# Another order for VectorE, ScalarE and GpSimd at both ends of the block products of a two-layer kernel

## The reference, cut to what matters

```
gate = sigmoid(x @ w_ple_gate)
x    = x + gate * (p_i @ w_ple_proj)
```

```
p = x @ w_in + b_in                     # a_u, a_v, q, k, v, r, a_low, g_a, g_b
v_n   = layer_norm(gelu(a_v))           # per token, over 1024 features
mixed = causal(w_s) @ v_n (per group of 128 features, chunks of 128 tokens) + b_s
y_a   = gelu(a_u) * mixed
log_f = log_sigmoid(a_low @ w_gate2 + b_gate) / 16
o     = gated linear attention(q, k, v, log_f), chunk by chunk
m     = sigmoid(g_a) * y_a + sigmoid(g_b) * norm(o) * silu(r)
h     = layer_norm(alpha * x + m @ w_out); then a feed-forward block of width 4096 with a second layer_norm
```

## Time and profile before

| | |
|---|---|
| median of 3 runs | 2411.16 us (2409.19 to 2412.22) |
| the profiled execution | 2408.89 us, span 2407.1 us |
| TensorE busy | 2324.1 us, 97% of the span, 12306 matmuls |
| weight loads (PEld) | 1884.6 us, 78% |
| VectorE | 1598.3 us, 66% |
| GpSimd | 1169.8 us, 49% |
| ScalarE | 890.7 us, 37% |
| mean DMA rate | 119 GB/s |
| mean granted TensorE clock | 0.986 of full speed |

### The profile page before, as it was taken

One profiled execution on the slowest core, in us unless ns is written; L12 is line 12 of the kernel. 1 busy time (PEld: TensorE's weight loads), 2 busy tenths in 40 slices (PEclk: granted clock), 3 DMA queues, 4 the chain that ended last, 5 costly groups with the idle time before them and its releaser, 6 DMA issues.

```text
span 2407.1 us, 33030 instructions
## 1 busy us (share of the span) xinstructions
PE 2324.1 (97%) x12306; PEld 1884.6 (78%) x12306; DVE 1598.3 (66%) x2066; ACT 890.7 (37%) x1383; POOL 1169.8 (49%) x699
## 2 busy tenths in 40 slices
PE   7999999999999997999899999999999999999996
PEld 5787777778888785778777877888877888888885
DVE  6657878876611648535677677646788666877788
ACT  4446454433200224453332232222263333444444
POOL 4355667673434535345323233344465555566665
PEclk9999999999999998999999999999999999999998
DMA  5333433436111352433222222222135444853322
GB/s 213 132 108 106 141 111 108 143 137 232 44 52 44 130 148 79 144 105 123 66 67 66 78 83 65 78 96 72 59 123 180 153 145 144 321 213 144 119 93 83
DMA packets 130087, 285.73 MB, mean 119 GB/s; under 512 B 13601, under 2 KB 49441, under 8 KB 125362
## 3 DMA queue, kind: packets, MB, share of 16 engines
q1 hardware_dynamic: 96672, 230.61, 27.6%
q10 hardware_dynamic: 33298, 53.56, 6.8%
HBM read 205.43 MB, written 78.72 MB: 118 GB/s over the span
## 4 chain that ended last, share of the span: by engine, by line
PE 45%; DVE 8%; issue 3%; DMA 2%; ACT 2%; POOL 1%; DVEq 0%; SPq 0%; ACTq 0%
PE pt L3702 15%; PE pt L3173 10%; PE wk L3702 6%; PE wk L3529 5%; PE pt L3529 3%; DMA eb<-o_d 1%; PE wk L3614 1%; PE wk L3713 1%; DVE darg L2708 1%; PE pt L3189 1%; DVE eb L2790 1%; PE wk L3647 1%; PE wk L3652 1%; PE wk L3648 1%; DVE ea L2792 0%
## 5 line engine op out<-in xcount | busy, mean ns | idle before, releaser
L833 POOL TENSOR_TENSOR w_hi<-w_raw,ones 128x1024 fp32r<-128x1024 f32 x70 | 137.0, 1957 | 548.1 <-PE pt L3173 510.5
L837 POOL TENSOR_TENSOR w_lo<-w_raw,w_hi 128x1024 fp32r<-128x1024 f32 x80 | 217.6, 2720 | 86.5 <-ACT w_hi L1107 65.5
L895 POOL TENSOR_TENSOR xl<-sraw,xh 128x512 fp32r<-128x512 f32 x80 | 137.5, 1729 | 81.0 <-ACT xh L1177 79.7
L976 POOL TENSOR_TENSOR wr_l<-raw,wr_h 128x512 fp32r<-128x512 f32 x80 | 137.1, 1717 | 79.5 <-ACT wr_h L1790 79.5
L3173 PE MATMUL pt<-h,w_hi 128*128 128x512 f32 x512 | 168.1, 410 | 1.2 <-DVE mix L2561 1.2
L3173 PE MATMUL pt<-l,w_hi 128*128 128x512 f32 x512 | 158.5, 391 | 0.0
L3173 PE MATMUL pt<-h,w_lo 128*128 128x512 f32 x512 | 158.3, 390 | 0.0
L948 POOL TENSOR_TENSOR l<-kq,h 128x512 fp32r<-128x512 f32 x64 | 88.5, 1393 | 112.7 <-ACT h L1481 112.7
L976 POOL TENSOR_TENSOR wr_l<-fraw,wr_h 128x512 fp32r<-128x512 f32 x60 | 79.9, 1335 | 90.9 <-ACT wr_h L1790 90.9
L3173 PE MATMUL pt<-xh,w_hi 128*128 128x512 f32 x384 | 119.5, 392 | 1.5 <-POOL w_lo L837 0.9
L3173 PE MATMUL pt<-xh,w_lo 128*128 128x512 f32 x384 | 118.7, 390 | 0.0
(11 more groups left out here) (667 smaller groups left out, 6755.0 us busy)
## 6 DMA issues: line engine op xcount, KB each, us to landing
w_raw<-ws_d SPq DMA_DIRECT2D x82, 512.0 KB, 3.5
fx_d<-stg SPq DMA_DIRECT2D x106, 256.0 KB, 2.8
sraw<-ws_d SPq DMA_DIRECT2D x32, 512.0 KB, 5.7
fraw<-ws_d SPq DMA_DIRECT2D x32, 512.0 KB, 5.0
raw<-ws_d SPq DMA_DIRECT2D x32, 512.0 KB, 8.7
kq<-ws_d SPq DMA_DIRECT2D x14, 1024.0 KB, 5.5
xs0f<-fx_d SPq DMA_DIRECT2D x10, 1024.0 KB, 4.9
xs1f<-fx_d SPq DMA_DIRECT2D x9, 1024.0 KB, 5.0
```

The costliest lines, as they stand in the source:

```text
L833: nc.gpsimd.tensor_tensor(out=w_hi[:, u, :], in0=w_raw[:, u, :], in1=zeros, op=ALU.add).then_inc(w_hi_done, 1)
L837: nc.gpsimd.tensor_tensor(out=w_lo[:, u, :], in0=w_raw[:, u, :], in1=w_hi[:, u, :].bitcast(f32), op=ALU.subtract).then_inc(w_split, 1)
L895: nc.gpsimd.tensor_tensor(out=lo, in0=sc_factor(n, SC_ORDER[i]), in1=hi.bitcast(f32), op=ALU.subtract).then_inc(sw_lo, 1)
L976: nc.gpsimd.tensor_tensor(out=low, in0=src, in1=high.bitcast(f32), op=ALU.subtract).then_inc(wl_done, 1)
```

## The change

No operation is added or removed, except that one wait of the mixing is taken at another count and three are added: ScalarE's last `eb` load and GpSimd's `split_pairs` now wait on `ln_ready`, and VectorE waits for its own last `mixed`. What moves:

- First seam, ScalarE: the load of `eb` for the last gate tile goes out when VectorE has read the old one; `quarter_hi(1)` and `(2)` stand ahead of `gate_high(KT - 2)`; `low_rank` stands ahead of all `piece_high`, and the loads of `wg2` are a function of their own behind `quarter_hi(11)`; `piece_high` and `quarter_hi` alternate.
- First seam, VectorE: the last gate tile is finished before `third_sum`; the first four `t_sum` stand before its low part; the memset of `alow` follows them; `t_sum` goes k by k; the rest of the sums is spread between the value steps.
- First seam, GpSimd: `second_low(k)` is spread between the weight lows 8 to 10.
- Logarithm units 0 and 1 are done at (2, 13) and (3, 7), the units 2 to 6 where 3 to 7 were, and unit 7 in product 13. The second operation of `z_min` is a function `z_less`, which for unit 0 is called later.
- Second seam: GpSimd's split waits for the first `norm_factors`; the memsets of `sc`, `kp` and `gst` stand before the mixing; the second half of the mixing takes the groups 4 to 7 first; and the first projection of the loop waits for the first ten groups that are emptied, not for all sixteen.

```diff
+LN_READY = 1
...
-    T_SUMS = [(n, 0) for n in ("T1", "T3", "T2", "T4")] + [(n, k) for k in range(1, 4) for n in ("T1", "T2", "T4")] + [
-        ("T3", k) for k in range(1, 4)]
+    MIXING = [(0, g) for g in range(KT)] + [(1, g) for g in (4, 5, 6, 7, 0, 1, 2, 3)]
+    T_SUMS = [(n, k) for k in range(4) for n in ("T1", "T3", "T2", "T4")]
...
         for g in range(28 * B_MATRICES):
+            if g == 8:
+                second_low(0)
+            if 8 <= g < 11:
+                second_low(g - 7)
             quarter_lo(g)
-            if g == 7:
-                for k in range(4):
-                    second_low(k)
+        pool.wait_ge(ln_ready, LN_READY + 1)
         split_pairs(S_G // 2, S_FF // 2)
...
-        def gate_load(i, u):
-            act.wait_ge(val_done, 3 * KT + i)
+        def gate_load(i, u, last=False):
+            act.wait_ge(*((ln_ready, 1) if last else (val_done, 3 * KT + i)))
...
         quarter_hi(0)
+        gate_load(KT - 1, 1, True)
+        quarter_hi(1)
+        quarter_hi(2)
         gate_high(KT - 2)
-        gate_load(KT - 1, 1)
         gate_tanh(KT - 1, 1)
-        for g in range(1, 4):
-            quarter_hi(g)
+        quarter_hi(3)
         gate_high(KT - 1)
         for g in range(4, 8):
             quarter_hi(g)
-        for n in range(4):
-            piece_high(n)
         low_rank()
-
+        piece_high(0)
+        piece_high(1)
+        quarter_hi(8)
+        piece_high(2)
+        quarter_hi(9)
+        piece_high(3)
+        quarter_hi(10)
+        quarter_hi(11)
+        gate_weights()
         for n in range(4, 8):
             piece_high(n)
...
-        quarter_hi(10)
-        quarter_hi(11)
         z_log(0)
-        quarter_hi(12)
-        quarter_hi(13)
+        quarter_hi(14)
+        quarter_hi(15)
+
+        quarter_hi(16)
+        quarter_hi(17)
         cu_store(0)
         z_log(1)
...
-        for e in range(11, 14):
+        for e in (11, 12):
             for q in range(4):
                 key_step(e, q)
+        z_log(7)
+        key_step(13, 0)
+        key_step(13, 1)
+        cu_store(7)
...
-        gate_add(KT - 2, 0, 16 * (KT // 2))
+        dve.wait_ge(evac_done, N_GATE + KT - 1)
+        dve.wait_ge(pp_in[0], 16 * (KT // 2))
+        STT(out=ea[:], in0=ea[:], scalar=1.0, in1=eb[:], op0=ALU.add, op1=ALU.mult).then_inc(ln_ready, 1)
+        dve.wait_ge(ln_ready, 1)
+        gate_sum(KT - 2)
+        gate_low(KT - 2)
...
+        gate_sum(KT - 1)
+        for n in range(4):
+            t_sum(n)
+        gate_low(KT - 1)
+        dve.wait_ge(kt_done, KT_DONE + 4)
+        nc.vector.memset(alow[0:RANK + 1, :], 1.0).then_inc(alow_set, 1)
         for s in range(4):
             third_sum(0, s)
-        gate_add(KT - 1, 1, 16 * (KT // 2))
-        for n in range(13):
-            t_sum(n)
-        nc.vector.memset(alow[0:RANK + 1, :], 1.0).then_inc(alow_set, 1)
         for s in range(4):
             second_sum(0, s)
-        for n in range(13, 16):
+        for n in range(4, 8):
             t_sum(n)
         for q in range(4):
             value_step(0, q)
+        for n in range(8, 16):
+            t_sum(n)
+        for q in range(4):
+            value_step(1, q)
 
         for s in range(4):
             fourth_sum(0, s)
-        for q in range(4):
-            value_step(1, q)
         for k in range(4):
             t_low("T3", k)
-        z_min(0)
         for q in range(4):
             value_step(2, q)
+        z_min(0)
         for k in range(4):
             t_low("T1", k)
-        z_min(1)
+        z_less(0)
         for s in range(4):
             first_sum(0, s)
-        z_min(2)
+        z_min(1)
+        z_less(1)
...
         norm_factors(0)
+        dve.wait_ge(k_bank, K_BANK + 4 * 20)
+        link(nc.vector.memset(sc[:], 0.0))
+        link(nc.vector.memset(kp[:], 0.0))
...
         statistics(20, 2)
+        dve.wait_ge(k_bank, K_BANK + 4 * 21)
+        link(nc.vector.memset(gst[:], 0.0))
         link(statistics(20, 3))
...
-        Z_AT = {(2, 0): 0, (2, 10): 1, (3, 4): 2, (6, 0): 3, (7, 0): 4, (9, 0): 5, (9, 10): 6, (10, 4): 7}
-        CU_AT = {(2, 9): 0, (3, 3): 1, (3, 13): 2, (6, 9): 3, (7, 9): 4, (9, 9): 5, (10, 3): 6, (10, 13): 7}
+        Z_AT = {(2, 13): 0, (3, 7): 1, (6, 0): 2, (7, 0): 3, (9, 0): 4, (9, 10): 5, (10, 4): 6, (13, 0): 7}
+        CU_AT = {(3, 6): 0, (3, 15): 1, (6, 9): 2, (7, 9): 3, (9, 9): 4, (10, 3): 5, (10, 13): 6, (13, 9): 7}
...
-        pe.wait_ge(mix_done, B_XT + 2 * KT)
+        pe.wait_ge(mix_done, B_XT + KT + 2)
```

More of the change, by code:

```diff
@@ L2628, in _ @@
             third_sum(2, s)
+        z_min(7)
+        z_less(7)
         for q in range(4):
@@ L2674, in _ @@
         dve.wait_ge(rg_done, 1 + B_SUMS)
-        for h in range(2):
-            for g in range(KT):
-                mixed(h, g)
-        dve.wait_ge(k_bank, K_BANK + 4 * 21)
-        link(nc.vector.memset(gst[:], 0.0))
-        link(nc.vector.memset(sc[:], 0.0))
-        link(nc.vector.memset(kp[:], 0.0))
+        for n in range(2 * KT):
+            mixed(n)
+        dve.wait_ge(mix_done, B_XT + 2 * KT)
         nc.vector.memset(qc[:], 0.0).then_inc(gst_done, 1)
```

92 lines of the change are left out of this document (51 added, 41 removed).

## The result

| | before | changed | ratio, 95% interval |
|---|---|---|---|
| first comparison, median | 2410.18 us (4 runs) | 2394.47 us (2392.63 to 2396.94, 4 runs) | 0.9935 [0.9919, 0.9951] |
| repeated later, median | 2407.47 us (17 runs) | 2389.93 us (2388.31 to 2394.74, 6 runs) | 0.9931 [0.9919, 0.9943] |
| profiled execution | 2408.89, span 2407.1 | 2392.79, span 2391.0 | |

A forecast was written before the change was run, and what follows sets the result against it. TensorE, busy 97% of the span, was taken as the bound, with the loss in its waits and low clock at two seams. Gains of 12 and 6 us, 18 together, took 2411.2 to 2393 us; 8-in-10 range 2384 to 2406.

The forecast's parts named there:

- (a): First seam: earlier `eb` load and rounding; operand sums start at about 907.8, 5.3 us earlier; 2.3 us `w_lo` wait goes.
- (b): First seam: `alow` copied ahead of the highs, done at 917.8; TensorE's 9.0 us wait goes, product runs to 927.4.
- (c): First seam: VectorE's list up to the first `z_less` puts `cu_rows` at 953.5; TensorE still loses some 9 us.
- (d): To the fourth product's end: second `cu_rows` late by 1.4, end at 966.5; first seam gains 12 us (2 to 16).
- list of signs: What the trace would show, including a 3 to 6 us wait under the first `cu_rows` and fifth product near 968.
- (e): Shifted logarithm units: unit 7 in product 14 covered with 0.9 us to spare; cost 0, at most 2 us.
- The second seam: First norm factors at 1172.5, not 1179.9; first projection at 1197.5, not 1204.7; gain 6 us, ends 2.5 and 8.
- (1): First seam: ScalarE's queue order and blocked VectorE give back 8 to 9 of 12 us; 2402; chance 0.20.
- (2): Clock stays at its upper level after remaining waits and quarter lows fit: 24 us gained, 2387; chance 0.18.
- (3): Third product: six GpSimd lows each held 5.6 us for 1.3, 26 us against 18 gained; 2419; chance 0.05.
- (4): `eb` load lands no earlier and unit 7 holds `key_add(13)`: gain under 5 us, 2408; chance 0.07.
- (5): Clock falls after waits at `cu_rows(0)` and the mixing: 4.9 us, about half already in the sum; 2395.5; chance 0.10.

The follow-up runs named there:

- Experiment 4: Changed kernel with ScalarE's copy of `alow` put behind `piece_high(0)` and `piece_high(1)`: 2398.29 us, ratio 0.9951 to before.
- Experiments 8 and 9: Changed kernel with four, then twelve, redundant operations more in VectorE's list ahead of `fourth_sum(0, s)`: 2390.93 us and 2401.55 us.
- experiment 7: Changed kernel with the first unit's store and second unit's logarithm ahead of rounding quarters 16 and 17 on ScalarE: 2386.83 us, ratio 0.9911.
- experiment 1: Changed kernel with the second seam's part undone, so the first seam alone: 2403.53 us, ratio 0.9965 to before.
- experiment 3: Changed kernel without GpSimd's wait for the first norm factors, so its split starts at once: 2402.36 us, ratio 0.996.
- experiment 6: Changed kernel with the memsets of `sc`, `kp` and `gst` between the mixing's second-half sums: 2390.36 us, ratio 0.9928.
- experiment 12: Changed kernel with the first projection waiting for all sixteen sums of the mixing, not ten: 2392.4 us, ratio 0.9936.
- experiment 10: Changed kernel unaltered, run again: 2389.93 us. Its table's left column: VectorE's product on the last gate load, in us after the first matmul.
- experiment 11: Changed kernel with quarter 1 rounded before the last gate load, the logarithm before two roundings, and memsets between the mixing's sums: 2388.59 us, ratio 0.9917.
- third group: The last four kernels sent together, on the same chip; the kernel before took 2407.47 us there.
- first group: The first four kernels sent together, on the same chip; the kernel before took 2410.86 us there.

## Why the prediction came out right, step by step

**(a) Last gate tiles: half right.** The operand sums began at 906.5 (forecast 907.8), since the last product ran at 903.95 and not at 905.2. The sentence on the rounding, at 899 at the latest and so 0.6 us into the first product, is the one that failed. In the list the rounding stands behind the issue of the last load, that waits for VectorE's product on the load before, and so for a DMA's landing. It held in the first profile (0.7 us into the product) and not in three others (2.2 to 4.1 us into it), with w_lo waits of 1.3 to 3.2 us where the earlier trace rows had 2.3. The change brought the rounding forward, but left it behind a landing.

**(b) The 9.0 us wait: right.** Copy at 915.9 to 917.8 (forecast 915.8 to 917.8), no wait, second product to 927.4 (927.4). Experiment 4 gives the price of such a wait: 7.2 us of it were worth 2.8 to 3.9.

**(c) VectorE's list: right in kind, 1.3 us too long.** First `cu_rows` at 951.05 for 953.5; one half of the difference is the earlier start, the other the list, which took 44.5 us from 906.5 for 45.8. TensorE lost 6.1 us between 927 and 953 (1.47 + 0.92 + 0.72 + 0.67 + 2.28), forecast 9; the wait at `cu_rows(0)` was 2.3 and not 3 to 6. Experiments 8 and 9 show the list as the bound: its measured length is paid one for one.

**(d) The second unit: mis-sized in terms that cancel.** Its wait was 2.4 us for 1.4, and experiment 7 shows that ScalarE's queue made it, as the step said. The step has the fifth product at 966.5 (965, and 1.5 for the clock); it began at 964.4, 2.1 us sooner because the first `cu_rows` was 2.5 sooner. (The "near 968" of the list of signs is another number: it counts the 2.05 us of the moved unit, which lie behind that start.) Against it the moved unit cost 2.4 and not 2.05, and 0.7 was lost at low clock behind the start (matmuls of 0.63 us where 0.39 is normal). The sum is 12.3 for 12.

**(e) Unit 7: right.** No wait in product 14.

**How much of the 12 is luck.** The 12.3 is one profile. Counted in the same way, the other profiles with this first seam unaltered give 11.8 (the changed kernel again), 8.6, 8.1, 14.3 and 9.5 us (experiments 1, 3, 6 and 12), and the runs of experiment 1 7.3 by the median, with the 12 outside their interval. They follow the left column of experiment 10's table: with the last load's product 4.5, 6.1, 6.3, 6.9, 8.5 and 10.6 us after the first matmul the seam gives 14.3, 12.3, 11.8, 9.5, 8.6 and 8.1. The forecast takes one landing as fixed, so that it hit this seam to 0.3 us is luck; 8 to 14 us is what it was worth in these six executions.

**The second seam: right.** With the two profiles laid over each other at the twenty-first product (12.88 us apart), the first factors were ready at 1172.4 (forecast 1172.5), the second at 1185.6 (1185.8), the restart came at 1188.9 (1189.4), the wait for `mix` was 3.63 (3.7). The projection started at 1198.6 for 1197.5. The reason is the clock: 6.34 us for 32 matmuls where 3.73 had been taken. The forecast's 6 of a computed 7.2 had room for it. (The chain of factors has thirteen operations behind the four aggregations, not fourteen.) Taking the memsets as free of GpSimd was right: the one of `kp` took 0.91 us wholly beside a split operation of 1.89, the one of `gst` 0.91 half beside another, and the same as in the kernel before with GpSimd idle (0.91 at 1204.4). Experiment 3 shows that the start of GpSimd's split is worth nearly this whole seam. The Trainium skill (SBUF — State Buffer, § Who interferes with whom) says that operations of VectorE with two SBUF inputs contend with a GpSimd instruction that reads SBUF and those with at most one, outside the two-port modes, do not. The trace agrees for the operations with both inputs in `sm`, which take 1.82 and 2.24 us in experiment 3, and for the memsets, with no input, which are not held at all. It leaves one open: the TENSOR_SCALAR of L1985, with one input, took 1.82 us beside GpSimd too, and no trace shows whether it ran in a two-port mode.

**The rivals.** (1) *Waits change their name*: half of it happened (`gz` 4.7 again, in two), but its 2402 lies outside the runs (2392.6 to 2396.9). Its 9 us for the first seam alone is near the 8.6 and 8.1 of experiments 1 and 3 and the 7.3 by time. (2) *More*: no. (3) *GpSimd starved*: no; the single lows of the third product took 1.3 to 1.7 us and the last four 6.37 together, none 5.6. (4) *No hold*: no. (5) *Clock at both waits*: it fell at the second `gz` wait, not at the first `cu_rows`, and at the mixing. Against the same matmuls at full clock that is 1.6 us (0.7 of it behind the start of the fifth product) and 2.6, 4.2 of the 4.9 named, of which the forecast held half. So of all rivals this one came nearest, and its 2395.5 is as near to the measured 2394.5 as the forecast's 2393. The Trainium skill (TensorE: Matmul & The Clock Gate, § HAM oscillation) has idle gaps put the array back to its lower clock. The traces here agree in kind, but not one for one: behind 2.63 us of wait 26 of the matmuls took 0.12 us each in experiment 6, and behind 2.64 us all 32 took 0.18 each in experiment 11.

**The end.** The projection came 19.0 us earlier for 18. The time given back later (2.9 us between projection and end) was not in the sum; why the clock is lower there stays open. The difference of the profiled execution to the median (2.3 in the forecast, 1.7 here) covered 0.6 of it. That the median came within 1.5 us of 2393 owes something to errors of opposite sign.

## What to carry to other kernels

A wait in a list is worth what is late behind it, not its length: of a wait for `alow` of 7.2 us about half was worth something. Before you price its removal, sum the list of the engine that made it, up to the next thing that the waiting engine needs. Where VectorE runs a chain of tiny operations whose result is awaited, hold GpSimd's large ones back until it is through; it cost one line and was worth 6 us by time, 7.2 in the trace. And look at what a moved instruction stands behind: a rounding behind the issue of a load takes over the spread of another load's landing. One profile doesn't show such a spread: compare several before you call a wait gone.

## What the runs showed of the hardware that was not expected

- A VectorE burst beside GpSimd has a price that is shared, not fixed: four sums took 6.01 us and the next four 2.50. Adding 2.4 us of operations lengthened the list by 0.3 to 1.3, adding 7.2 by 9.7 to 10.8, depending on where it is measured from.
- After idle times of the same length (2.63 and 2.64 us) at the same place the granted clock was 1.00 once and 0.75 once (windows of 5 us); before the first cumulative sum, after 2.28 us the eight matmuls took 1.13 us in the changed kernel, and after 2.29 us 2.05 in experiment 1. What decides wasn't settled.
- The landing of the gate's loads moves by some microseconds between executions with the same code, and the third group's chip ran the kernel before 3.4 us faster than the first group's.
